# Block sums of the down weights moved from the feed-forward on GpSimd to the input projection on VectorE, and last stores of three stages issued by SyncE

## The reference

```python
z = rms_norm(x, norm_attn_g) @ w_in                # 2304 columns: q, k, v 512 each; gating 512; state space 256
y_attn = dilated_attention(q, k, v, rel_bias)      # 8 heads, three (window, dilation) branches
y_sgu  = spatial_gating(z[..., 1536:2048], ...)    # chunks of 128
y_ssm  = s5_ssm(z[..., 2048:], ...)                # 16 groups, 64 complex states
mix = concatenate([rms_scale(y_attn), rms_scale(y_sgu), rms_scale(y_ssm)]) * branch_norm_g
h = x + mix @ w_out
u = conv_width_3(rms_norm(h, norm_ffn_g) @ w_up) + conv_b   # 5632 columns: values and gates
h = h + (gelu(gate) * val) @ w_down                # w_down is 2816 x 1024
h = h + sigmoid(rms_norm(h, norm_ple_g) @ w_gate) * (p @ w_proj)
out = rms_norm(h, final_norm_g)
```

## Time and profile before

| | |
|---|---|
| median of 3 runs | 2734.63 us (2733.23 to 2735.4) |
| profiled execution | 2732.35 us, its span 2730.7 us |
| mean granted clock of TensorE, of full speed | 0.97 |
| TensorE busy | 2540.4 us (93%), 13619 matmuls |
| VectorE busy | 1815.3 us (66%) |
| ScalarE busy | 1351.2 us (49%) |
| GpSimd busy | 825.0 us (30%) |
| moved by transfers | 420.98 MB, 154 GB/s |
| hardware queue, software queue (GpSimd's) | 39.7% and 8.7% of the 16 DMA engines' time |

### The profile page before, as it was taken

How to read it: one execution, slowest core, us unless ns; L and a number is a source line. 1 busy time by engine, 2 the same in 40 slices (tenths; PEclk the granted TensorE clock), 3 DMA queues, 4 the chain that set the end, 5 groups by cost and what they waited for, 6 DMA issues and landing times. The chain is left out here.

```text
span 2730.7 us, 38614 instructions
## 1 busy us (share of the span) xinstructions
PE 2540.4 (93%) x13619; PEld 2184.8 (80%) x13619; DVE 1815.3 (66%) x3351; ACT 1351.2 (49%) x2435; POOL 825.0 (30%) x627
## 2 busy tenths in 40 slices
PE   6999998999976799689999989999999999998998
PEld 4889897999965688578788878888888877886876
DVE  2113186677757777589999966768898975563433
ACT  3343432666643666545555545545555553344544
POOL 2454553666610111235555540001222220000000
PEclk9999999999998899899999999999999999998999
DMA  4665544888663255124444477553332336752221
GB/s 160 198 221 170 168 149 135 189 185 190 141 183 121 79 188 192 60 94 161 158 159 143 162 266 262 185 177 97 101 112 97 108 134 236 277 203 108 81 75 43
DMA packets 311084, 420.98 MB, mean 154 GB/s; under 512 B 22914, under 2 KB 222914, under 8 KB 306155
## 3 DMA queue, kind: packets, MB, share of 16 engines
q1 hardware_dynamic: 285018, 330.06, 39.7%
q0 software_dynamic: 25888, 88.63, 8.7%
HBM read 298.59 MB, written 124.16 MB: 155 GB/s over the span
## 5 line engine op out<-in xcount | busy, mean ns | idle before, releaser
L2646 PE MATMUL ffn_bank<-ffn_x,ffn_ring 128*128 128x512 f32 x704 | 276.5, 393 | 16.6 <-DVE ffn_strips L2446 10.7
L2648 PE MATMUL ffn_bank<-ffn_x,ffn_ring 128*128 128x512 f32 x704 | 275.6, 392 | 0.0
L2647 PE MATMUL ffn_bank<-ffn_x,ffn_ring 128*128 128x512 f32 x704 | 275.4, 391 | 0.0
L2714 POOL DMA_DIRECT2D ffn_act<-ffn_late x154 | 85.7, 558 | 473.8 <-DVE ffn_late L2478 443.0
L1124 POOL TENSOR_TENSOR in_w_lo<-in_w,in_w_hi 128x2048 fp32r<-128x2048 f32 x36 | 168.0, 4665 | 181.0 <-ACT in_w_hi L1001 181.0
L2646 PE MATMUL ffn_bank<-tail_shared,ffn_ring 128*128 128x512 f32 x528 | 206.9, 392 | 9.1 <-DVE ffn_ring L2421 7.5
L594 ACT ACTIVATE att_exps<-att_scores,att_part 128x256 f32<-128x256 f32 (+1 forms) x384 | 153.0, 454 | 117.0 <-DVE att_part L561 114.1
L2648 PE MATMUL ffn_bank<-tail_shared,ffn_ring 128*128 128x512 f32 x528 | 206.4, 391 | 0.0
L561 DVE CUSTOM_DVE_ANT_0 att_scores<-att_bank,att_bias 128x256 f32<-128x256 f32 (+1 forms) x384 | 122.7, 363 | 95.7 <-PE att_bank L504 85.9
L1094 PE MATMUL in_bank<-in_w_hi,in_hi 128*128 128x256 f32 x640 | 183.1, 286 | 0.7 <-issue 0.7
L1095 PE MATMUL in_bank<-in_w_lo,in_hi 128*128 128x256 f32 x640 | 181.8, 284 | 0.0
(11 more groups left out here) (384 smaller groups left out, 7378.8 us busy)
## 6 DMA issues: line engine op xcount, KB each, us to landing
ffn_w<-in_ffn_w_up SPq DMA_DIRECT2D x88, 512.0 KB, 4.9
ffn_act<-ffn_late POOLq DMA_DIRECT2D x154, 256.0 KB, 2.3
in_w<-in_w_in SPq DMA_DIRECT2D x36, 1024.0 KB, 6.3
ffn_a_raw<-ffn_act SPq DMA_DIRECT2D x77, 256.0 KB, 4.0
ffn_a_raw_later<-ffn_act SPq DMA_DIRECT2D x77, 256.0 KB, 4.4
ffn_w<-ffn_down_sums SPq DMA_DIRECT2D x16, 1024.0 KB, 5.5
ffn_w<-in_ffn_w_down SPq DMA_DIRECT2D x12, 1024.0 KB, 5.5
ffn_pieces<-in_ffn_w_down POOLq DMA_DIRECT2D x44, 256.0 KB, 3.7
```

Source lines behind the costliest of these rows:

```text
L2646: pe.matmul(out[:, :], hi[:, k], x_hi[kind][:, k], start=(k == 0 and fresh), stop=False, skip_group_check=not fresh)
L2647: pe.matmul(out[:, :], hi[:, k], x_lo[kind][:, k], start=False, stop=False, skip_group_check=not fresh)
L2648: mm = pe.matmul(out[:, :], lo[:, k], x_hi[kind][:, k], start=False, stop=(k == KH - 1), skip_group_check=not fresh)
```

## The change

The sums of `w_down` blocks leave the feed-forward and are made in the input projection, in blocks 2 to 23, one step of the 22 in each. The `pieces` buffer lies where `bias_rows` of the projection was, so its first load waits for `lines_stored`. GpSimd loads the four blocks of a step at the end of the block before (`load_pieces`), and stores the summed ones behind the weight split of the step's block, ahead of its result splits (`store_pieces`). VectorE makes the four subtractions (`sum_pieces`): those of the first three blocks of a group ahead of `scale_rows` of the next group, of the fourth and fifth behind it, of the others each behind two of the `split_x`. The feed-forward loses the loads, sums, stores and waits; `tap_rows` gets a buffer of its own there.

The last two tile stores of mixing, the last quarter of the feed-forward (`store_last`) and the last tile of the output are issued by SyncE, with semaphores that outlive the stage where the next stage waits for them. GpSimd's waits at the ends of mixing and of the output stage go; in the feed-forward SyncE waits for the stores of `h1` before it loads the second half's rows, and in the last stage SyncE waits for the last stores.

```diff
--- before.py
+++ after.py
...
+        self.h1_stored, self.h1_last_stored = keep.sems("h1_stored", 2), keep.sem("h1_last_stored")
...
-        self.row_loaded, self.h2_stored = keep.sem("row_loaded"), keep.sem("h2_stored")
+        self.row_loaded, self.h2_stored, self.h2_last_stored = (keep.sem(n) for n in ("row_loaded", "h2_stored", "h2_last_stored"))
...
+    FH = w_down.shape[0] // P // 2
+    T_COLS, T_STEPS, T_FROM = BANK // 2, 2 * FH, 2
+    down_blocks = w_down.rearrange("(b f p) (n c) -> p b f n c", p=P, b=2, n=D // BANK)
...
+        pieces = st.over("pieces", [P, 4, T_COLS], F32, nc.sbuf_base - NB * BAND * 4)
...
+            def sum_pieces(B):
+                n = B - T_FROM
+                if not 0 <= n < T_STEPS:
+                    return
+                b11, b12, b21, b22 = (pieces[:, m] for m in range(4))
+                dve.wait_ge(t_loaded, 2 * (n + 1) * DMA)
+                nc.vector.tensor_tensor(b11, b12, b11, ALU.subtract).then_inc(t_summed, 1)
+                dve.wait_ge(t_summed, n * 4 + 1)
+                nc.vector.tensor_tensor(b12, b22, b12, ALU.subtract).then_inc(t_summed, 1)
+                dve.wait_ge(t_summed, n * 4 + 2)
+                nc.vector.tensor_tensor(b22, b22, b11, ALU.subtract).then_inc(t_summed, 1)
+                dve.wait_ge(t_summed, n * 4 + 3)
+                nc.vector.tensor_tensor(b21, b21, b22, ALU.subtract).then_inc(t_summed, 1)
...
             for g in range(1, G):
+                first = (g - 1) * NBLK
+                for b in range(LOOK - 1):
+                    sum_pieces(first + b)
                 scale_rows(g)
+                for b in range(LOOK - 1, LOOK + 1):
+                    sum_pieces(first + b)
                 for k in range(KC):
                     split_x(g, k)
+                    if k % 2:
+                        sum_pieces(first + LOOK + 1 + k // 2)
                 if g == G - 2:
                     parameters.compute_exponentials(dve)
             parameters.compute_powers(dve)
...
+            def pieces_of(n):
+                i, half = divmod(n, 2)
+                return i, slice(half * T_COLS, (half + 1) * T_COLS)
+            def load_pieces(n):
+                i, cols = pieces_of(n)
+                if n:
+                    pool.wait_ge(t_stored, n * DMA)
+                else:
+                    pool.wait_ge(lines_stored, DMA)
+                for b in range(2):
+                    pool.dma_start(pieces[:, 2 * b:2 * b + 2], down_blocks[:, b, i, :, cols]).then_inc(t_loaded, DMA)
+            def store_pieces(n):
+                i, cols = pieces_of(n)
+                pool.wait_ge(t_summed, n * 4 + 4)
+                pool.dma_start(down_sums[:, :, i, cols].rearrange("k p c -> p k c"), pieces[:, :, :]).then_inc(t_stored, DMA)
             split_w(0)
             for g, b, B in blocks():
                 if B + 1 < G * NBLK:
                     split_w(B + 1)
+                if 0 <= B - T_FROM < T_STEPS:
+                    store_pieces(B - T_FROM)
                 for u in units_of(B):
                     if is_qk[u]:
                         split_result(u)
+                if 0 <= B + 1 - T_FROM < T_STEPS:
+                    load_pieces(B + 1 - T_FROM)
+            pool.wait_ge(t_stored, T_STEPS * DMA)
...
-        loaded, stored = st.sems("loaded", RING), st.sems("stored", 2)
+        loaded, stored = st.sems("loaded", RING), rows_ahead.h1_stored
...
             for t in range(rows_ahead.tiles):
                 sp.wait_ge(stored[t % 2], (t // 2 + 1) * DMA)
                 sp.dma_start(rows_ahead.rows[:, t], h_tiles[t]).then_inc(rows_ahead.loaded[t], DMA)
+            for j in range(RING - 2, RING):
+                sp.wait_ge(added, steps * RING * HALVES - (RING - 1 - j) * HALVES)
+                sp.dma_start(h_tiles[(steps - 1) * RING + j], result[j % 2][:, :]).then_inc(rows_ahead.h1_last_stored, DMA)
...
                     if j + 3 < RING or not last:
                         normalise_gate(i, j + 3)
+                    if last and j >= RING - 2:
+                        continue
                     pool.wait_ge(added, i * (RING * HALVES) + (j + 1) * HALVES)
...
             run(pool, step)
-            for s in range(2):
-                pool.wait_ge(stored[s], steps * RING // 2 * DMA)
...
-        pieces = st.sb("pieces", [P, 4, T_COLS])
-        tap_rows = st.over("tap_rows", [2 * F, N_TAPS, P], F32, nc.sbuf_base - 4 * T_COLS * 4)
+        tap_rows = st.sb("tap_rows", [2 * F, N_TAPS, P])
...
                     if kind in W_SUM:
-                        if h == 0:
-                            sp.wait_ge(t_stored, 2 * (fs[-1] + 1) * DMA)
                         src = down_sums[W_SUM[kind], :, fs[0]:fs[-1] + 1]
...
+            def store_last():
+                h, p = HALVES - 1, PASSES - 1
+                first = h * PART + BANK
+                sp.wait_ge(added, added_through(h, p))
+                sp.dma_start(h2[first:first + BANK, 0:BANK].rearrange("(t p) n -> p t n", p=P),
+                             resid[h][0][:, :, :]).then_inc(ahead.h2_last_stored, DMA)
...
                             sp.wait_ge(act_ready, (h + 1) * F * TG)
+                            for h1_stored in rows_ahead.h1_stored:
+                                sp.wait_ge(h1_stored, (T // P // 2 - 1) * DMA)
+                            sp.wait_ge(rows_ahead.h1_last_stored, 2 * DMA)
                             load_rows(h + 1, 0)
...
+            store_last()
...
-            def load_pieces(n):
-                i, half = divmod(n, 2)
-                cols = slice(half * T_COLS, (half + 1) * T_COLS)
-                if n:
-                    pool.wait_ge(t_stored, n * DMA)
-                else:
-                    pool.wait_ge(taps_turned, 1)
-                for b in range(2):
-                    pool.dma_start(pieces[:, 2 * b:2 * b + 2], down_blocks[:, b, i, :, cols]).then_inc(t_loaded, DMA)
-            def sum_pieces(n):
-                i, half = divmod(n, 2)
-                cols = slice(half * T_COLS, (half + 1) * T_COLS)
-                b11, b12, b21, b22 = (pieces[:, m] for m in range(4))
-                pool.wait_ge(t_loaded, 2 * (n + 1) * DMA)
-                nc.gpsimd.tensor_tensor(b11, b12, b11, ALU.subtract).then_inc(t_summed, 1)
-                pool.wait_ge(t_summed, n * 4 + 1)
-                nc.gpsimd.tensor_tensor(b12, b22, b12, ALU.subtract).then_inc(t_summed, 1)
-                pool.wait_ge(t_summed, n * 4 + 2)
-                nc.gpsimd.tensor_tensor(b22, b22, b11, ALU.subtract).then_inc(t_summed, 1)
-                pool.wait_ge(t_summed, n * 4 + 3)
-                nc.gpsimd.tensor_tensor(b21, b21, b22, ALU.subtract).then_inc(t_summed, 1)
-                pool.wait_ge(t_summed, n * 4 + 4)
-                pool.dma_start(down_sums[:, :, i, cols].rearrange("k p c -> p k c"), pieces[:, :, :]).then_inc(t_stored, DMA)
...
             sum_last()
             for h in range(HALVES):
                 for i in range(FH):
-                    if h == 0:
-                        load_pieces(2 * i)
                     store_act(h, i, 0, 0)
-                    if h == 0:
-                        sum_pieces(2 * i)
                     store_act(h, i, 1, 0)
                     sum_early(h, i)
-                    if h == 0:
-                        load_pieces(2 * i + 1)
                     store_act(h, i, 0, 1)
-                    if h == 0:
-                        sum_pieces(2 * i + 1)
                     store_act(h, i, 1, 1)
                     sum_late(h, i)
                 for n in range(STORES):
-                    store(h, n)
+                    if (h, n) != (HALVES - 1, STORES - 1):
+                        store(h, n)
             pool.wait_ge(stored, (HALVES * STORES - 1) * DMA)
...
-            sp.wait_ge(ahead.h2_stored, h2_stores * DMA)
+            sp.wait_ge(ahead.h2_stored, (h2_stores - 1) * DMA)
+            sp.wait_ge(ahead.h2_last_stored, DMA)
...
+            sp.wait_ge(result_ready, steps * RING)
+            sp.dma_start(out_tiles[T // P - 1], result[LAST % 2][:, :]).then_inc(last_stored, DMA)
+            for s in range(2):
+                sp.wait_ge(stored[s], (steps * RING // 2 - s) * DMA)
+            sp.wait_ge(last_stored, DMA)
...
-            with pool.Fori(0, steps) as i:
-                for j in range(RING):
+            def step(i, last):
+                for j in range(LAST if last else RING):
                     pool.wait_ge(result_ready, i * RING + (j + 1))
                     pool.sem_inc(st.pool_passed, 1)
                     pool.dma_start(out_tiles[bass.ds(i * RING + j, 1)].rearrange("a p d -> (a p) d"), result[j % 2][:, :]).then_inc(stored[j % 2], DMA)
-            for s in range(2):
-                pool.wait_ge(stored[s], steps * RING // 2 * DMA)
+            run(pool, step)
```

11 lines of the change are left out of this document (6 added, 5 removed).

## The result

The changed kernel takes 2790.76 us (median of 4 runs, 2787.63 to 2792.34) against 2733.93 before. The ratio is 1.0206, with a 95% interval of 1.0188 to 1.0224: 2.1% or some 57 us slower. The forecast was 2747, with a range of 2740 to 2756 of its own and of 2731 to 2768 with its rivals. Both are missed.

The account below looks back on a forecast made before the run. TensorE was taken to set the time. Projection +36, feed-forward -9 and last stores -14.7 gave +12.3: 2744.7 us on the profiled execution, 2747 as median, range 2740 to 2756, or 2731 to 2768 with rivals.

Parts of the forecast that it names:

- the loop on GpSimd: Input projection: weight split, sums, handover, store landing and load issues take 11.7 us per block, alone costing about nothing.
- From store to next load, 3.66: Input projection: from the start of a step's store to the start of the next loads takes 3.66 us.
- landing takes 1.3 us longer: Projection's upper bound: transfers meeting weight loads lengthen each stall and the loop by 1.3 us, about 16 more, 52.
- The wait for the sums, 1.99: Input projection: VectorE's four sums take 1.84 us per step, plus about 0.15 for the handover to GpSimd.
- The three stalls behind scale_rows, 6.8 each: Blocks 3, 12 and 21: sums behind scale_rows hold GpSimd, so TensorE stalls 6.8 us each time, 20.3 together.
- Block 20, 4.6: Projection: sums in block 18 stand behind the state-parameter chain, so TensorE stalls 4.6 us when block 20 should start.
- The clock, 9.4: Projection: TensorE's lower clock after stalls costs 2.6 us for each long one and 1.6 for the shorter, 9.4.
- Band tables: Input projection, first group: mentioned as also written there, in a rival about late weights, with no price of their own.
- Feed-forward, -9: Feed-forward's first half: removing 88 GpSimd subtractions and 66 transfers gains 9 us, bounds 5 and 12.
- The last stores, -14.7: Ends of mixing, feed-forward and output: stores issued by SyncE gain 4.3, 8.0 and 2.4 us, bounds 7 and 16.
- The rule of the Trainium skill: Stage ends: another issuer saves at most half a microsecond per issue, 1.5 together, putting the whole near 2760.
- The third rival: Input projection: transfers are the bound, landing a good microsecond later and weights late in first group; 2763 us; 15 in 100.

Follow-up runs that it names:

- four-buffer kernel: Changed kernel with four buffers for the pieces, loads two steps ahead, stores one block later, fourth block's sums ahead of scale_rows: 2737.16 us, 4.4 over before.
- second profile of before: The kernel before, unchanged, profiled again: 2733.18 us, with 410.23 us from the fourth eviction of the feed-forward's first half to the last.
- two buffers alone: Changed kernel with two buffers for the pieces used in turn, same bytes, sums and queue places: 2763.86 us, 31.1 over before.
- 11.5 for the tables: Kernel with four buffers for the pieces, its eight band tables written in blocks 24 to 31 in place of 1 to 8: 2725.54 us, 7.1 under before.
- no sums at all: Kernel before with the last stores on SyncE and sums made nowhere, plain w_down blocks read instead, so output differs: 2712.67 us, 21.7 under before.
- with the sums moved: Changed kernel with the last stores back on GpSimd, so only the sums moved: 2802.27 us, 69.6 over before.

## Why the prediction was wrong

The direction was right. The failed term is the loop on GpSimd. "The sum is 4.62 + 1.84 + 0.15 + 3.66 + 1.44 = 11.7 us" and "Alone this loop costs about nothing": it was 15.7 us over 20 blocks, and 14.4 without the waits behind scale_rows, above the mean block of 11.7, so it set the pace of the stage. The terms that were too small in it are the landing of the store, 3.66, and the wait for the sums, 1.84 + 0.15. With the measured waits put in, the loop gives the time: 20 x 11.7 by the prediction is 234; the landings add 36.6, the sums 16.4 and the three waits behind scale_rows 27.1, together 314, and the trace has 314.4 from the split of block 3 to that of block 23, where before it was 235.0.

Point by point (the first three are the loop's; what follows on the clock is time inside it, not beside it, so the points do not add up to the 78.7):

- **From store to next load, 3.66.** Measured 3.44 to 3.46 in eight of the 21, in seven of which the result splits hid the landing, but 4.6 to 8.0 in the others; mean 5.39, so 21 x 1.73 = 36 us over the stage. The 3.66 was read in the feed-forward, where the weight loads are of 512 KB. In the projection a load of 1 MB goes out on SyncE at or soon after the end of a weight split, and the store comes 0.8 to 3.6 us behind it in blocks 14 to 17. The run with that load held, and with it what SyncE had behind it, shows these transfers as the cause there, without parting them. That in the first group it is the tables is argued from their place. I had taken one price from a quieter stretch, and as upper bound "landing takes 1.3 us longer", worked from mean DMA shares (0.55 against 0.46). The mean hid that the store's rivals come at the same moment as the store. The "about 16 more" is too little even by its own terms: 1.3 us in each of 22 steps is 28.6, so the bound would have been near 65 and not 52. Here the Trainium skill's page "DMA: Bandwidth & Descriptors", section "Issuing engines are not separate DMA queues", which I had weighed against the last stores, bears on the projection: transfers of all engines run on the same DMA engines and interleave, and these traces agree (7.30 and 3.46 us).
- **The wait for the sums, 1.99.** In the 19 places without row scaling it was 1.97 to 5.61, mean 3.13, so 19 x 1.14 = 22 us. In 13 of the 19 the loads of a step landed after the end of the split that was to hide them; in block 13, issued at 244.93, they landed at 253.2, and the split ended at 250.9. Of the 22, 16 fall in the 20 blocks above.
- **The three stalls behind scale_rows, 6.8 each.** Measured 7.75, 6.50 and 8.74, together 23.0 against 20.3, and the store stood 10.9, 10.75 and 11.4 us for the sums, where I wrote "about 10". Setting the order right gave 18.7 us, where 20.3 and 7.8 of clock were forecast. This part was right in place and mechanism, and near in price.
- **Block 20, 4.6.** Not there as such: the gap is 1.01, with 2.90 ahead of block 19. The store of block 18 did wait 4.36 us for the sums, 2.4 above the 1.97 of the quickest, so the mechanism shows and the price does not.
- **The clock, 9.4.** The matmuls took 24.0 us longer. I counted four long gaps; there were 17, and behind eleven of them, down to 2.79 us, the clock was lower. But in the loop's account above there is no place for the 24.0: while GpSimd sets the pace, a quicker TensorE would have waited longer for the next split. That is worked out from this sum; no run changed the clock alone.
- **Band tables.** Named in a rival in half a sentence, not priced. They cost 14 to 15 us in the first group of the four-buffer kernel, together with the steps.
- **Feed-forward, -9.** The stage from VectorE's drain of mixing to its own got 10.1 us shorter, of which 4.6 is the end of mixing: 5.5. The last stores alone went with a first half 3.9 us shorter (2.5 against the second profile of before), and removing the sums with 2.9 more. By the medians it is 3.1 to 4.7. The term was mis-sized, at its lower bound of 5 or under it; a half that has the same work "without them" is not what removing them gives.
- **The last stores, -14.7.** 15.0 by the drains (4.6, 8.1 and 2.3 against 4.3, 8.0 and 2.4), 17.0 by the run. The rule of the Trainium skill that the prediction weighed against this part (page "DMA: Bandwidth & Descriptors", section "Issuing engines are not separate DMA queues"), read strictly, would have left 1.5. In the feed-forward, where GpSimd did not wait for its last store before either, the 8.1 is the length of its drain. In mixing the edit also takes the wait for the landing out of the stage (3.1 us from issue to drain before), and no run parts that from the change of engine.

The sum by the stage ends in the trace: 78.7 for the projection, 1.5 in the stages up to the end of mixing, less 5.5 and 15.0, is 59.7 of the 60.0. The third rival was nearest in mechanism ("Transfers are the bound in the projection": landings late, weights late in the first group) at 52 for the projection; it was given 15 in 100. Its sign "distances between blocks are above 12.5 us everywhere" is what the trace shows in all but two of the 20 periods (11.5 to 21.5, mean 15.7).

By the runs, each against the kernel before of its set, the way down from the changed kernel is: 18.7 us for the order, 33.7 for the chain of waits (four buffers, earlier loads and late stores, not tested one by one; two buffers alone gave 25.7, with the old order), 11.5 for the tables, and 14.6 from there to the kernel with no sums at all. Of the last piece 13.3 lie in the projection by the two profiles (last split at 452.98 and 439.71). It is not broken down by a run. That it is VectorE's row scaling stretched by GpSimd's work and the extra transfers is argued from gaps and rows, not shown. Since no sums at all is worth 3 to 5 us over the last stores alone, the most that moving them could pay is about that.

## What to carry to other kernels

A free engine is not a free chain: before hanging a load, an operation and a store onto an engine that feeds the bound one, add up the landings of the transfers in that stretch, and ask which other transfer the same event releases. Price a landing where the work will stand, not where it stood, and first measure what taking the work away altogether would give. Where another engine's chain sets the pace of the bound one, its own slower clock may lie inside the chain's time: do not add it to the stalls without asking. The end of a stage can wait for the drain of the engine that issued the last store: here the last stores of three stages, issued by SyncE in GpSimd's place, gave 17 us of 2733, of which 8.1 are the feed-forward's drain.

## What the runs showed of the hardware that was not expected

- A VectorE operation of 128x1024 that meets GpSimd's arithmetic is held for nearly the whole of it: four scalings took 2.74 us alone, and 7.48 across a weight split of 4.54, with one of them at 5.43 in place of 0.75. The Trainium skill, page "SBUF — State Buffer", section "🔬 SBUF: two separate sides", says that of a GpSimd operation and a VectorE operation in a two-port mode or with two inputs in SBUF, the one that starts first holds the shared port for its whole instruction and the other waits; the difference of 4.74 us agrees with that.
- GpSimd's drain right behind its last store, of 1 MB, was 8.13 us, 8.12 in the second profile and 7.80 with the sums moved; SyncE's in its place was 0.12. In mixing and output, where GpSimd had waited for the landing, its drain was 1.36 and still last.
